# A gather ring of 5 slots instead of 10, with the projection's buffers beside it

## The reference

```python
def blk(xb):
    q = (xb @ w_q).reshape(PEER_BLOCK, PEER_HEADS, 2, PEER_DK // 2)
    s1 = jnp.einsum('thd,hnd->thn', q[:, :, 0], keys[0])
    s2 = jnp.einsum('thd,hnd->thn', q[:, :, 1], keys[1])
    v1, i1 = lax.top_k(s1, PEER_TOPK)
    v2, i2 = lax.top_k(s2, PEER_TOPK)
    cand = (v1[..., :, None] + v2[..., None, :]).reshape(...)
    cidx = (i1[..., :, None] * PEER_NK + i2[..., None, :]).reshape(...)
    sc, pos = lax.top_k(cand, PEER_TOPK)
    eidx = jnp.take_along_axis(cidx, pos, axis=-1)
    g = jax.nn.softmax(sc, axis=-1)
    act = jax.nn.gelu(jnp.einsum('thkd,td->thk', u[eidx], xb))
    return jnp.einsum('thk,thkd->td', g * act, v[eidx])
```

## Time and profile before

| | us |
|---|---|
| median of 3 runs | 4599.99 (4595.82 to 4603.43) |
| profiled execution, span | 4588.8 |
| PE busy | 3744.7 (82%) |
| DVE busy | 3181.0 (69%) |
| POOL busy | 1511.0 (33%) |
| ACT busy | 967.0 (21%) |
| HBM read | 1462.84 MB, 320 GB/s over the span |

### The profile page before, as it was taken

One profiled execution on the slowest core, in us unless ns is written; L12 is line 12 of the kernel. 1 busy time (PEld: TensorE's weight loads), 2 busy tenths in 40 slices (PEclk: granted clock), 3 DMA queues, 4 the chain that ended last, 5 costly groups with the idle time before them and its releaser, 6 DMA issues. The chain is left out here.

```text
span 4588.8 us, 42624 instructions
## 1 busy us (share of the span) xinstructions
PE 3744.7 (82%) x10383; PEld 1787.6 (39%) x10383; DVE 3181.0 (69%) x7667; ACT 967.0 (21%) x2243; POOL 1511.0 (33%) x1316
## 2 busy tenths in 40 slices
PE   7688888878787878788877988878787878787877
PEld 2266565333333333333333544333333333333332
DVE  6533343778777777777887353778778778787787
ACT  5432141111111111111122341111111111111112
POOL 0000000344444444444443000344444444444443
PEclk9899869989899999899998999989898989898999
DMA  8410004999999999999997104899999999999998
GB/s 330 177 48 28 34 0 171 360 412 384 408 399 396 401 396 398 397 397 399 406 414 315 59 27 166 348 411 377 402 393 391 404 390 404 388 407 384 401 420 351
DMA packets 206990, 1467.85 MB, mean 320 GB/s; under 512 B 24280, under 2 KB 29160, under 8 KB 35688
## 3 DMA queue, kind: packets, MB, share of 16 engines
q0 software_dynamic: 184320, 1342.26, 72.3%
q1 hardware_dynamic: 21684, 121.29, 7.0%
q10 hardware_dynamic: 828, 2.76, 0.2%
HBM read 1462.84 MB, written 3.38 MB: 320 GB/s over the span
## 5 line engine op out<-in xcount | busy, mean ns | idle before, releaser
L785 PE MATMUL peer_acc<-peer_ring,peer_diag 128*128 128x512 f32 x5120 | 2505.4, 638 | 634.6 <-DVE peer_diag L651 634.3
L438 POOL DMA_INDIRECT peer_ring<-in_uv,peer_index x1280 | 1498.7, 1171 | 2515.2 <-PE peer_acc L785 1738.2
L785 PEld LDWEIGHTS peer_acc<-peer_ring,peer_diag 128*128 128x128 f32 x5120 | 988.5, 202 | 1923.4 <-issue 1000.8
L643 DVE CUSTOM_DVE_ANT_0 peer_ring<-peer_ring,HY 128x1024 f32<-128x1024 f32 x1280 | 1557.9, 1218 | 139.1 <-issue 62.5
L509 ACT ACTIVATE peer_acts<-peer_dots 128x1 f32<-128x1 f32 x1280 | 258.6, 203 | 2793.2 <-DVE peer_dots L643 2792.6
L651 DVE TENSOR_SCALAR peer_diag<-ident,peer_acts,peer_gate 128x128 f32<-128x128 f32 x1280 | 438.0, 342 | 61.9 <-PE peer_acc L785 42.2
L738 PE MATMUL peer_qp<-HT,peer_wq 128*128 128x512 f32 (+1 forms) x896 | 294.9, 453 | 0.0
L738 PEld LDWEIGHTS peer_qp<-HT,peer_wq 128*128 128x128 f32 x896 | 182.4, 204 | 241.3 <-issue 241.3
L564 DVE MAX8 peer_best<-peer_sc 128x8 f32<-128x128 f32 x160 | 40.3, 289 | 331.9 <-PE peer_sc L753 331.4
L657 DVE TENSOR_TENSOR peer_tmp<-peer_acc,peer_G 128x1024 f32<-128x1024 f32 x80 | 98.0, 1224 | 91.2 <-PE peer_acc L785 84.8
L702 PE MATMUL peer_acc<-peer_ring,HY 128*128 128x512 f32 x320 | 142.6, 607 | 15.7 <-DMA peer_ring<-in_w_out 15.7
(11 more groups left out here) (280 smaller groups left out, 2958.9 us busy)
## 6 DMA issues: line engine op xcount, KB each, us to landing
mod_wmod<-in_w_mod SPq DMA_DIRECT2D x16, 2048.0 KB, 8.9
peer_ring<-in_uv,peer_index POOLq DMA_INDIRECT x1280
HT<-in_w_mod SPq DMA_DIRECT2D x8, 2048.0 KB, 9.2
peer_wq<-in_w_q SPq DMA_DIRECT2D x16, 1024.0 KB
peer_ring<-in_w_out SPq DMA_DIRECT2D x8, 1024.0 KB, 8.8
lru_wlru<-in_w_lru SPq DMA_DIRECT2D x4, 2048.0 KB, 7.7
hgrn_wqvg<-in_w_hgrn_qvg SPq DMA_DIRECT2D x4, 1536.0 KB, 6.5
peer_ring<-scratch_mod_rows SPq DMA_DIRECT2D x12, 512.0 KB, 14.3
```

What stands on the lines that cost most here:

```text
L438: pool.indirect_dma_start(ring[:, j % SLOTS, :], None, uv[:, :], bass.IndirectOffsetOnAxis(ap=index[:, j:j + 1], axis=0), element_offset=l ...
L643: dve.tensor_tensor_reduce(u, u, H[:, j // TOPK, :], 1.0, 0.0, ALU.mult, ALU.add, dots[:, j:j + 1]).then_inc(dot_done, 1)
L785: last_mm = pe.matmul(acc[b % 2][:, lo:lo + 512], diag[:, j % NDIAG, :], ring[:, j % SLOTS, D + lo:D + lo + 512], start=(e == 0), stop=(e ...
```

## The change

`SLOTS` goes from 10 to 5. `w_out`, `AB` and `G1` get memory of their own; `squares` goes to `qN`, which is free then; `nextAB` is now the same memory as `AB`, so its load in layer 0 waits until all five blocks are normalized. GpSimd's two waits `FREE` and `NORM` are gone. VectorE's wait for `next_in` moves from the start of the expert stage to the first use.

```diff
-SLOTS = 10
+SLOTS = 5
...
         ring = sb("ring", [P, SLOTS, 2 * D])
 
-        FREE, NORM = 2, 6
-        w_out = ring[:, FREE:NORM, :].rearrange("p s (k n) -> p (s k) n", n=D)
-        AB = ring[:, NORM:NORM + 2, :].rearrange("p s (c d) -> p s c d", c=2)
-        G1 = ring[:, NORM + 2, :].rearrange("p (c d) -> p c d", c=2)
-        squares = ring[:, NORM + 3, 0:D]
+        w_out = sb("w_out", [P, KD, D])
+        AB = sb("AB", [P, 2, 2, D])
+        G1 = sb("G1", [P, 2, D])
...
-            nextAB = sb("nextAB", [P, 2, 2, D])
+            nextAB = AB
...
+        squares = qN[:, :, :].rearrange("p a t -> p (a t)")[:, 0:D]
...
                 else:
+
+                    sp.wait_ge(h_ready, NB)
                     load_mod(sp, io, nextAB[:, 0, :, :], layer + 1, 1, next_in)
                     load_mod(sp, io, nextAB[:, 1, :, :], layer + 1, 0, next_in)
...
                     for j in range(PER_HEAD):
-                        if j == FREE:
-
-                            pool.wait_ge(projected, NB)
-                        if j == NORM:
-
-                            pool.wait_ge(h_ready, NB)
                         if j % TOPK == 0:
...
                     if n >= NB and final:
+                        if n == NB:
+                            dve.wait_ge(next_in, 16)
...
                     gain_shift = nextAB if n >= NB else AB
+                    if n == NB:
+                        dve.wait_ge(next_in, 64)
...
                 dve.wait_ge(g2_in, 32)
-                dve.wait_ge(next_in, 16 if final else 64)
```

## The result

The changed kernel takes 5394.35 us (median of 4 runs, 5390.03 to 5407.81), the kernel before, on the same chip, 4598.69 us (4 runs, 4595.82 to 4603.43). The ratio is 1.173, with a 95% interval of 1.1712 to 1.1749. The forecast of 5100 us had the direction; the loss is 796 us, not 500, and 5394 lies above the upper end of the range, 5310.

What follows compares the result with a forecast made beforehand. Transfers were taken to bind most of the time; with five slots a head is 122.05 + 43q, 241.6 us at q = 2.78, 245.4 with the clock, 31.2 more than 214.2, giving 5100 us, range 4870 to 5310.

Steps and rivals of the forecast that it cites:

- What bounds the kernel: In the expert stages transfers bind most of the time, VectorE and TensorE nearly as long; ten slots let them run apart.
- Projection and loads: Output projection's own memory, later loads of the next layer's rows and moved waits: together 0, bounds -2 and +5 us.
- The loop of the ring: Gather j waits for weighted sum j - 5: 10.0 us for four gathers, 2.50 each, no slack.
- One unit of 16: Dot 1 to dot 8 keeps VectorE full, 19.84 or 22.24 us, gathers in time; then nine steps at the loop's pace.
- Head boundary: From dot 79 to the next head's dot 0 12.1 us, and 1.15 to dot 1.
- The clock: TensorE's slow first sums after idling add 1.8 us at the head boundary and 0.5 for each of four units.
- q: Pace of the loop per gather from dot 8 of a unit on, taken as 2.78 us between 2.48 and 3.07.
- The rule against the trace: Skill's rule: 1 MiB per DMA gives full bandwidth, so short queues cost nothing; the trace's short-queue stretch shows 3.07 us per gather.
- (a): Transfers keep full rate, 2.48 us a gather, and the clock costs nothing: about 4830 us; chance 0.18 with neighbourhood.
- (b): TensorE's clock falls in the units' second half too, every sum 1.8 us longer: 5410 us; chance 0.17.
- (c): Faster: scores are there when VectorE asks, up to 233 us won, 4367 us, if gathers keep below 2.68 us; chance 0.03.
- (d): No change: five slots cover the routing, or the queue was never deeper: 4600 us; chance 0.03.

Runs made afterwards that it cites:

- The kernel that has only the depth: The kernel before, with its ten slots and layout, but only five gathers may be outstanding: 5395.49 us, ratio 1.1719.
- The bare loop: Gather, dot, activation, weight and sum only, the rest of the kernel left out: 2.74 us a step waiting on the sum five before, 2.54 six, 2.51 ten.
- half the bytes: The changed kernel, but each gather fetches rows of 1024 numbers instead of 2048: 4832.73 us, ratio 1.0508.
- early-scores kernel: The kernel before, ten slots, but TensorE makes the scores of the unit after next behind sum 10 of a unit: 4526.87 us, ratio 0.9845.

## Why the prediction was wrong

By its own steps, in their order:

**What bounds the kernel: right.** Ten slots were what held three nearly equal resources apart, and the loss shrinks with each slot that is taken back.

**Projection and loads, 0 us: right.** The kernel that has only the depth gives the same time (5395 and 5394).

**The loop of the ring: right in kind, one term mis-sized.** This is the step that failed. Over dots 10 to 16 of the units (476 dots in 14 heads, and VectorE waited for the landing before each of them) the loop takes 12.3 us on average, not 10.0. Its terms, as averages: the sum's end 4.23 us after the dot behind which the weight stands (forecast 3.43; of these sums 98 stand right behind query matmuls, and 64 begin while the granted clock is at the 1.2 GHz level), 0.85 to the issue (0.78), the issue 1.18 (1.17), and from its end to the dot 6.05, where I had put 4.63. So 1.4 of the 2.3 us lie in the transfer and 0.8 in the sum. A quarter of 12.3 is 3.08, and the mean step is 3.05.

The 4.63 is real, but it is the time of a gather that finds the engines idle. In the changed kernel 58 gathers found no other on its way at their issue's end, and they landed after 4.66 us on average. Of the 476 gathers above, 30 found none and landed after 4.62 us, 210 found one other (5.34) and 234 found two (6.80). So half of them stand behind two others in the loop that they are meant to serve. Issues at an even 3.05 us, each landing after 4.6, would find just one. The sentence that failed is therefore "slots are freed at an even pace here". That the uneven pace makes the queue is read from these groups; it wasn't varied by itself.

The bare loop shows that 4.7 can hold (2.48 a step) as long as nothing is late, and that without slack a late landing isn't won back (2.74 on average). The kernel around it, with its routing pauses, longer issues and query matmuls, brings it to 3.05; this share is the remainder of the two measurements, and how it divides among them was not tried. I took the middle of 2.48 and 3.07. The row of the short queue, 3.07, lies beside the measured 3.05; whether that stretch had the same cause isn't shown.

**One unit of 16: the first half too small.** I forecast 19.84 us in unit 0 and 22.24 in the others, 108.8 in all, with every gather of this stretch in time. Measured: 21.81, 24.60, 23.69, 25.53, 24.33, in all 120.0. With half the bytes they add up to 111.7, with six gathers in use to 111.7 and with seven to 111.5. So 2.9 us of the difference lay in taking 22.24 from one unit for all four, and 8.3 are waits for landings in between the pieces of routing: before dots 2 to 8 VectorE is idle 10.3 us a head, with seven 2.4. I had seen 0.8 us of it for unit 0, and left it out.

**Head boundary, 13.25: right** (12.87). **The clock, 3.8 us: counted twice.** The slow sums are there, but they lie in the measured steps.

The sum of a head, forecast 245.4: +11.2 for the first halves, +9.8 for 36 steps at 3.05 instead of 2.78, +1.3 for the seven of unit 4 at 2.97, -0.4 for the boundary, -3.8 for the clock make 263.5. Sixteen times 18.1 is 290 us, and 5100 + 290 is the time measured. So about half of the miss was q, and about half was that I held the first halves free of waits; both are the loop turning more slowly than forecast.

**The rule against the trace.** The trace was right. One gather of 1.05 MB outstanding reached 181 GB/s, two 350, three 402. That at least 1 MiB per DMA gives full bandwidth, which the Trainium skill, "DMA: Bandwidth & Descriptors", states in its rules for kernel authors, holds here only with three of them under way.

**The rivals.** (a) fell: 2.48 is reached only where the weight doesn't wait behind a dot, or nothing is late. (b) gave nearly the right time (5410) for a reason that isn't there: in the second half shown above the clock was at 1.00, and in the two expert stages it stood at the 1.2 GHz level for 673 of 4197 us, 16%, against 516 of 3395, 15%, before. With its time at 5410 it would have looked confirmed by the time alone; the clock's column refutes it. The clock did fall once sums were halved. (c) was half right: the scores were there when VectorE asked (21.2 us), and nothing was won, as the heads were far above its 2.68 us a gather. In the early-scores kernel, at ten slots, the same change was worth 71 us. (d) fell.

## What to carry to other kernels

Once the landed slots are used up, the pace of a ring is the length of its loop over the slots minus what the loop holds by program order, here one; put the transfer into that loop with the queue before it, as it is under load, and not as it is when the engines are idle. If the quotient comes out equal to the transfer itself, there is no slack, and a late landing is lost for good. Here one slot more was worth 463 us, the weight moved in front of the next dot for half of each unit 172, and half the columns of nearly every sum 96. And a rival whose time fits isn't confirmed until the row that it names has moved.

## What the runs showed of the hardware

- Gathers of 1.05 MB (128 rows of 8 KB): 5.8 us each with one outstanding, 2.9 with two, 2.5 with three or more; scattered and regular rows are alike. From the issue's end to the landing, with nothing else running, 4.6 us on average with one or two outstanding, 6.3 with three, 8.7 with four.
- GpSimd's issue of an indirect gather took 0.94 us when VectorE was idle, whatever TensorE did, and 1.4 to 1.5 us on average, 1.9 at most, while VectorE worked.
- With its sums halved, TensorE's granted clock fell to 0.72 on average over a stage, where it was 0.92 with whole sums; the gain was 96 us instead of the nearly 200 expected.
